# A two-layer decoder trunk: X by two DMA queues, a new plan for the convolution's taps, one sum in layer 1's norm

## The chip, the cores and the metric

One core of one Trainium2 chip runs the whole computation. The metric is the device time of one execution in microseconds; lower is better. The times are of three runs of the kernel before, and the profile is of one more execution.

## The reference

x is 256 tokens by 1024 channels, float32. Two layers, both with a residual.

```python
# layer 0
h = rms_norm(x, norm0_g)
a, bv, bg, z = split(h @ w_in0)            # 1024, 1024, 1024, 2048 columns
ya = (multiscale_pool(a) @ pool_w per group) * pool_scale
u  = causal_depthwise_conv(bv * sigmoid(bg), conv_w, 31 taps) + conv_b
yb = silu(layer_norm(u, cnorm_g, cnorm_b))
x  = x + (concat(ya, yb) * silu(z)) @ w_out0
# layer 1
h = rms_norm(x, norm1_g)
q, k, v, z = split(h @ w_in1)              # 4 x 1024 columns
q, k = rms_norm per head of 64, q * 64 ** -0.5
o = softmax(q k' - slope * distance, causal) v   # 16 heads; 256 tokens are one block
x = x + (o * silu(z)) @ w_out1
```

rms_norm divides by sqrt(mean(x * x) + 1e-6) over the 1024 channels.

## The kernel before, in words

**Units.** All weights come as 49 units of 128 x 2048 float32 (1 MB) in the order of use: 0 to 7 the gate and value of the convolution in turn, 8 to 11 the pooling channels, 12 to 15 and 17 to 20 the SiLU gates of layer 0 (`ZB`, `ZA`), 16 the pooling weights (`PW`), 21 to 28 the output projection (`OA`, `OB`), 29 to 32 the gate of layer 1 (`Z1`), 33 to 44 k, q and v in pairs, 45 to 48 the last projection. A float32 product is made of three fp32r matmuls: weights and activations are cut into a rounded high part (`w_hi`, `h_hi`, by ScalarE, `cut_hi`, L461) and the rest (`w_lo`, `h_lo`, by VectorE, `cut_lo`, L740), and `product` (L1077 to L1079) adds hi*hi, hi*lo and lo*hi. Five units, `NATIVE`, are multiplied uncut in float32, and the low part of four units, `ADDED`, is made by an accumulating DMA that GpSimd issues (L426) after ScalarE has written minus the high part.

**Buffers and queues.** `raw` holds four units. SyncE issues the loads in order (L399), each as soon as the unit four before it has been cut. w_hi and w_lo hold four cuts. Each engine runs one fixed instruction list, and semaphores order them. X (128 partitions x 8 tiles of 256) comes first on SyncE's queue, in two DMAs of four tiles each (L388), the units follow, and the parameters (149 KB, norm gains and convolution taps) go by ScalarE's queue (L494).

**Start.** TensorE runs 12 warm-up matmuls on a tile of ones (L1145). ScalarE squares X by pairs of tiles, TensorE adds the squares over partitions by eight matmuls with the ones (L1154), ScalarE takes the root, VectorE the reciprocal (`take_inverse`). Before that VectorE multiplies X by the gain (`gained`, L746), and unit 0 works on this product, without the reciprocal; its result is scaled late (`late_gate`, `scale_late`, named in `EARLY`). Unit 1 is the first to need the normed h.

**Convolution.** 31 taps on 8 tiles of channels run on VectorE in the slots of units 2 to 21, placed ahead of time by `conv_plan`: a tap is either one multiply-add of VectorE a tile (L856), or a product that ScalarE makes for two tiles (L548) and VectorE adds (L860), or, for two pairs, an accumulating DMA of GpSimd. The planner goes slot by slot with a budget: the unit's length less what `slot_work` says that each engine has to do there already; it gives a product to ScalarE where its budget is over 0.8. The products of late slots live in a ring of four. After the last tap VectorE folds eight tiles into one (L873), TensorE adds over partitions (L1200, `MEAN_AT`), VectorE centres (L880), ScalarE squares (L469), VectorE folds again (`fold`, L767), and TensorE makes the sum at `SUM2_AT` (L1154). ScalarE casts unit 26 ahead of these squares.

**Layer 1's norm.** As the last projection of layer 0 closes two tiles at a time, VectorE adds the residual (L961), applies the gain (L746) and makes the low part (`low_h(1, m)`, L753); ScalarE squares (L469) and makes the high part (L487). In the loop over `Z1`, units 29 and 30 work on the h without the reciprocal, in ya_hi and ya_lo, and are scaled late; unit 31 is the first that needs `over_rms`, which norms H and cuts it again. The sum over partitions is four matmuls inside unit 29: after step k = 1 the two tiles that hold folded pairs, after k = 2 the two last tiles unfolded.

## Time and profile before

| | us |
|---|---|
| median of 3 runs (lowest to highest) | 329.43 (329.25 to 330.02) |
| the profiled execution | 329.37 |
| its span, first to last instruction | 327.4 |
| TensorE busy (matmul / weight load) | 321.8 / 295.5 |
| VectorE busy | 261.1 |
| ScalarE busy | 235.8 |
| GpSimd busy | 51.2 |
| TensorE's granted clock, mean | 0.999 of full |

The span is what the profile covers; the execution's own time has some 2 us around it. A row of the timeline gives start, length, engine, line, what is written from what, and how many instructions are merged into it; the brackets give idle time before it and who ended it. A float32 matmul has two records, an fp32r matmul one.

### The profile page before, as it was taken

Reading aid. Unit: us, or ns where it says so; the run is one execution under the profiler, and the core shown is the slowest. Engines: PE = TensorE matmul, PEld = TensorE weight load, DVE = VectorE, ACT = ScalarE, POOL = GpSimd, SP = SyncE. Lnnn points to the kernel's source line nnn. Section 1 sums busy time; section 2 is a strip of 40 time slices with the busy share of each in tenths; the row PEclk is TensorE's granted clock in tenths of the full one; section 3 lists DMA queues with packets and bytes.
Section 4 is the critical chain, followed back from the end, with each engine's and each line's share of the span. In section 5 each row is a group of like instructions: output and inputs, shape, how many; then the busy total and the mean of one; then the engine's idle time right before and its main releaser. Section 6 shows DMA issues by size and latency. Waiting matters only on the chain.

```text
span 327.4 us, 5849 instructions
## 1 busy us (share of the span) xinstructions
PE 321.8 (98%) x2244; PEld 295.5 (90%) x2244; DVE 261.1 (80%) x482; ACT 235.8 (72%) x436; POOL 51.2 (16%) x58
## 2 busy tenths in 40 slices
PE   8999999999999999998999999999999999999995
PEld 8899999999999999997999999988887777778885
DVE  2799989999999999999895898846556887758533
ACT  4687999997999889987766557814756667566630
POOL 0050024423224112120000000005500231400000
PEclk9999999999999999999999999999999999999999
DMA  7988478969999699984539244780635323200003
GB/s 275 413 278 355 156 265 224 203 148 344 346 328 214 122 411 292 217 270 93 249 143 397 104 148 152 279 322 13 243 130 166 132 103 129 114 2 0 2 0 130
DMA packets 12843, 64.79 MB, mean 198 GB/s; under 512 B 1424, under 2 KB 1552, under 8 KB 6544
## 3 DMA queue, kind: packets, MB, share of 16 engines
q1 hardware_dynamic: 8064, 53.78, 43.3%
q0 software_dynamic: 4608, 10.49, 17.7%
q8 instruction: 18, 0.29, 0.4%
q10 hardware_dynamic: 144, 0.15, 0.2%
q14 instruction: 9, 0.07, 0.1%
HBM read 52.88 MB, written 1.05 MB: 165 GB/s over the span
## 4 chain that ended last, share of the span: by engine, by line
PE 90%; ACT 4%; DVE 3%; issue 1%; POOL 0%; DVEq 0%; ACTq 0%; POOLq 0%
PE bank L1077 24%; PE bank L1078 23%; PE bank L1079 23%; PE bank L1111 4%; PE bank L1137 3%; PE bank L1185 2%; PE bank L1291 2%; PE bank L1318 2%; PE bank L1154 2%; PE bank L1145 2%; PE bank L1304 2%; ACT scratch L548 1%; DVE scratch L856 1%; ACT w_hi L461 1%; PE bank L1270 1%
## 5 line engine op out<-in xcount | busy, mean ns | idle before, releaser
L740 DVE TENSOR_TENSOR w_lo<-raw,w_hi 128x1024 fp32r<-128x1024 f32 x80 | 95.3, 1222 | 16.9 <-ACT w_hi L461 16.7
L461 ACT CAST w_hi<-raw 128x1024 fp32r<-128x1024 f32 x88 | 88.6, 1047 | 7.5 <-DMA raw<-w 3.8
L1077 PE MATMUL bank<-h_hi,w_hi 128*128 128x256 f32 x320 | 91.1, 285 | 0.0
L1079 PE MATMUL bank<-h_hi,w_lo 128*128 128x256 f32 x320 | 90.5, 283 | 0.0
L1078 PE MATMUL bank<-h_lo,w_hi 128*128 128x256 f32 x320 | 90.5, 283 | 0.0
L1078 PEld LDWEIGHTS bank<-h_lo,w_hi 128*128 128x128 f32 x320 | 61.4, 192 | 0.1
L1077 PEld LDWEIGHTS bank<-h_hi,w_hi 128*128 128x128 f32 x320 | 61.4, 192 | 0.1
L1079 PEld LDWEIGHTS bank<-h_hi,w_lo 128*128 128x128 f32 x320 | 61.4, 192 | 0.0
L856 DVE SCALAR_TENSOR_TENSOR scratch<-scratch,params 128x256 f32<-128x256 f32 x106 | 43.4, 482 | 0.2
L1077 PE MATMUL bank<-ya_hi,w_hi 128*128 128x256 f32 x144 | 42.6, 296 | 0.0
L1078 PE MATMUL bank<-ya_lo,w_hi 128*128 128x256 f32 x144 | 40.7, 282 | 0.0
L1079 PE MATMUL bank<-ya_hi,w_lo 128*128 128x256 f32 x144 | 40.7, 282 | 0.0
L1077 PE MATMUL bank<-w_hi,h_hi 128*128 128x512 f32 x96 | 39.2, 408 | 0.0
L1078 PE MATMUL bank<-w_lo,h_hi 128*128 128x512 f32 x96 | 37.6, 391 | 0.0
L1079 PE MATMUL bank<-w_hi,h_lo 128*128 128x512 f32 x96 | 37.5, 391 | 0.0
L548 ACT ACTIVATE scratch<-scratch,params 128x256 f32<-128x256 f32 x78 | 32.8, 504 | 0.0
L435 POOL DMA_DIRECT2D side_v<-side_ring x24 | 21.0, 905 | 73.9 <-ACT side_ring L528 52.8
L1077 PEld LDWEIGHTS bank<-ya_hi,w_hi 128*128 128x128 f32 x144 | 27.5, 191 | 2.0 <-issue 1.7
L1078 PEld LDWEIGHTS bank<-ya_lo,w_hi 128*128 128x128 f32 x144 | 27.5, 191 | 0.1
L1079 PEld LDWEIGHTS bank<-ya_hi,w_lo 128*128 128x128 f32 x144 | 27.5, 191 | 0.0
L860 DVE TENSOR_TENSOR scratch<-scratch 128x512 f32<-128x512 f32 x39 | 26.1, 690 | 1.0
L446 POOL TENSOR_SCALAR scratch<-scratch 128x8 f32<-128x8 f32 x8 | 5.1, 632 | 116.5 <-DVE scratch L1037 116.2
(106 smaller groups left out, 522.2 us busy)
## 6 DMA issues: line engine op xcount, KB each, us to landing
raw<-w SPq DMA_DIRECT2D x49, 1024.0 KB, 6.9
side_v<-side_ring POOLq DMA_DIRECT2D x24, 256.0 KB, 6.5
w_lo<-raw POOLq DMA_DIRECT2D x8, 512.0 KB, 7.3
X<-xT SPq DMA_DIRECT2D x2, 512.0 KB, 5.2
out<-X SPq DMA_DIRECT2D x4, 256.0 KB, 2.6
consts<-const SPq DMA_DIRECT2D x1, 290.0 KB, 13.3
params<-vec ACTq DMA_DIRECT2D x1, 149.0 KB, 4.9
```

Source lines behind the costliest of these rows:

```text
L435: pool.dma_start(side_v[:, pair, item % 2, :, :], side_home(pair, item), accum_op=ALU.add).then_inc(side_added[pair][item % 2], 16)
L461: nc.scalar.copy(halves(w_hi, cut_slot(n), half), halves(raw, n % RAW, half)).then_inc(hi_cut, 1)
L548: last = nc.scalar.mul(product_home(product)[:, i, :], U[:, c, k:k + S], column(CW + TAPS * c + k))
L740: nc.vector.tensor_tensor(halves(w_lo, cut_slot(n), half), halves(raw, n % RAW, half), halves(w_hi, cut_slot(n), half).bitcast(F32), ALU.s ...
L856: nc.vector.scalar_tensor_tensor(V[:, c, :], U[:, c, k:k + S], column(CW + TAPS * c + k), V[:, c, :], ALU.mult, ALU.add).then_inc(tap, 1)
L860: nc.vector.tensor_tensor(V[:, c:c + 2, :], V[:, c:c + 2, :], product_home(product), ALU.add).then_inc(tap, 1)
L1077: nc.tensor.matmul(dst, wh, ah, start=start, stop=False, skip_group_check=True)
L1078: nc.tensor.matmul(dst, wh, al, start=False, stop=False, skip_group_check=True)
L1079: return nc.tensor.matmul(dst, wl, ah, start=False, stop=stop, skip_group_check=True)
L1111: last = nc.tensor.matmul(dst, wr, (H if n else H0)[:, k, :], start=start, stop=stop, skip_group_check=True)
L1137: return nc.tensor.matmul(dst, wr, SZ[:, (KD if n in OB else 0) + tile, :], start=start and m % 2 == 0, stop=stop, skip_group_check=True)
L1145: nc.tensor.matmul(bank[7][:, 0:P], ones[:, :], ones[:, :], start=True, stop=True, skip_group_check=True)
```

## The change

X comes in two DMAs by partition halves, one issued by SyncE, one by ScalarE, on one semaphore; each partition's 8 KB is one piece. The parameters are issued by ScalarE after its half. Both engines wait for all of X. The warm-up has 10 matmuls. In the planner `ZA[3]` is given 1.2 less of VectorE work, `PW` 0.8 less of ScalarE work, and from `ZA[3]` on products go to ScalarE only after four entries of the slot. Layer 1's squares are folded to one tile, in two parts, and summed by one matmul after k = 5. Unit 31 joins the units that work without the reciprocal. Unit 32's high cast, and those of 33 and 34, come sooner in ScalarE's list; VectorE cuts 33 and 34 before unit 31's late gate.

```diff
--- before.py
+++ after.py
@@ -57,7 +57,7 @@
 EARLY_ADDED = (10,)
 ADDED = EARLY_ADDED + (21, 22, 24)
 SPARE = 22
-WARM = 12
+WARM = 10
 RAW = 4
 CUT = 4
 
@@ -123,6 +123,8 @@
     return sum(1 for n in units[:i] if n not in NATIVE)
 
 
+
+SQUARE_FOLDS = (0, 2, 2, 2), (0, 4, 2, 3), (0, 6, 2, 4), (0, 1, 1, 4)
 
 STEPS = 48
 CUT_HI_AT, CUT_LO_AT = (1, 7, 9, 15), (2, 8, 11, 15)
@@ -185,8 +187,10 @@
         dve, act = dve + 0.8, act + 0.6
     if n in BG or n in A or n in ZB or n in ZA:
         act += 0.6
+    if n == ZA[3]:
+        dve -= 1.2
     if n in (ZB[0], PW):
-        act += 0.7 if n == ZB[0] else 1.6
+        act += 0.7 if n == ZB[0] else 0.8
     return dve, act
 
 
@@ -212,7 +216,7 @@
                 late = len(used)
             free = pair < (n - 1) // 2
             last_ones = n == OA[0] and sum(map(len, left.values())) <= LAST_PRODUCTS
-            if last_ones or act_time > 0.8 and free and n < OA[0] and n + 3 != SPARE:
+            if last_ones or act_time > 0.8 and free and n < OA[0] and n + 3 != SPARE and (n < ZA[3] or len(plan[n]) >= 4):
                 count += 1
                 plan[n].append((tiles, k, len(used), max(last.get(c, 0) for c in tiles), count))
                 used.append(count)
@@ -239,8 +243,9 @@
 
 
 MEAN_AT = 2, 0, 5
+SUM3_AT = 5
 SUM2_AT = 3, 0, 2
-EARLY = (BG[0],), (Z1[0], Z1[1])
+EARLY = (BG[0],), (Z1[0], Z1[1], Z1[2])
 
 
 def hybrid_trunk(nc, xT, w, vec, const, out):
@@ -326,7 +331,7 @@
         TR, SC, PV = bank[4], (bank[5], bank[6]), bank[7]
 
 
-        x_in = [sem(f"x_in{i}") for i in range(2)]
+        x_in = sem("x_in")
         vec_in, const_in, stored = sem("vec_in"), sem("const_in"), sem("stored")
         raw_in = [sem(f"raw_in{i}") for i in range(RAW)]
         ones_set, pads_set, qs_set = sem("ones_set"), sem("pads_set"), sem("qs_set")
@@ -384,8 +389,7 @@
 
         @block.sync
         def _(sp):
-            for i in range(2):
-                sp.dma_start(X[:, 4 * i:4 * i + 4, :], xT[:, 4 * i:4 * i + 4, :]).then_inc(x_in[i], 16)
+            sp.dma_start(X[0:P // 2, :, :], xT[0:P // 2, :, :]).then_inc(x_in, 16)
             for n in range(NU):
                 m = n - RAW
                 if m >= 0:
@@ -491,12 +495,13 @@
                 act.wait_ge(late, layer + i + 1)
                 nc.scalar.activation(dst, dst, func).then_inc(done, 1)
 
+            act.dma_start(X[P // 2:P, :, :], xT[P // 2:P, :, :]).then_inc(x_in, 16)
             act.dma_start(V_[:, :], vec).then_inc(vec_in, 16)
             act.wait_ge(ones_set, 2)
             prime(ACT.Sqrt)
             for m in range(4):
-                if m % 2 == 0:
-                    act.wait_ge(x_in[m // 2], 16)
+                if m == 0:
+                    act.wait_ge(x_in, 32)
                 square(0, m, X)
             take_root(bank[4], 1)
             prime(ACT.Sigmoid)
@@ -625,10 +630,13 @@
                 high_h(1, m)
             cut_hi(Z1[1])
             take_root(bank[0], 3)
+            prime(ACT.Silu)
             cut_hi(Z1[2])
+            cut_hi(Z1[3])
             for m in range(4):
                 high_h(2, m)
-            cut_hi(Z1[3])
+            cut_hi(KU[0])
+            cut_hi(KU[0] + 1)
 
             def head_exp(h):
 
@@ -665,8 +673,6 @@
                             heads_hi(4 * octet + i)
 
             for i, n in enumerate(Z1):
-                if i > 1:
-                    cut_hi(n + 2)
                 to = SZ1[:, 2 * i:2 * i + 2, :]
                 if n in EARLY[1]:
                     late_gate(1, i, to, ACT.Silu, sz1_ready)
@@ -755,14 +761,12 @@
 
             folds = 0
 
-            def fold(group, pairs):
+            def fold(group, first, last):
 
                 nonlocal folds
-                steps = ((0, 2, 2), (0, 4, 2), (0, 6, 2), (0, 1, 1)) if pairs == 4 else ((0, 2, 2), (0, 4, 2))
-                for i, (a, b, n) in enumerate(steps):
-                    if i < 3:
-                        dve.wait_ge(sq_ready, 4 * group + i + 2)
-                    if i:
+                for a, b, n, squares in SQUARE_FOLDS[first:last]:
+                    dve.wait_ge(sq_ready, 4 * group + squares)
+                    if first or (a, b) != SQUARE_FOLDS[first][:2]:
                         dve.wait_ge(folded, folds)
                     nc.vector.tensor_tensor(SQ[:, a:a + n, :], SQ[:, a:a + n, :], SQ[:, b:b + n, :],
                                             ALU.add).then_inc(folded, 1)
@@ -795,8 +799,8 @@
 
             dve.wait_ge(vec_in, 16)
             for m in range(4):
-                if m % 2 == 0:
-                    dve.wait_ge(x_in[m // 2], 16)
+                if m == 0:
+                    dve.wait_ge(x_in, 32)
                 gained(0, m)
             take_inverse(1)
             normed_h(0, 0)
@@ -914,7 +918,7 @@
                     low_ya(i)
 
             centre()
-            fold(1, 4)
+            fold(1, 0, 4)
             cut_lo(OB[1], (0,))
             take_inverse(2)
             dve.wait_ge(sq_ready, 8)
@@ -967,10 +971,12 @@
                     residual(m, 0)
                     dve.wait_ge(x_updated, m + 1)
                     gained(1, m)
+                if m == 4:
+                    fold(2, 2, 4)
                 if m:
                     low_h(1, m - 1)
                 if m == 2:
-                    fold(2, 3)
+                    fold(2, 0, 2)
             cut_lo(Z1[1])
             take_inverse(3)
             cut_lo(Z1[2])
@@ -1025,11 +1031,11 @@
                         if s == values[i] + 3:
                             heads_lo(4 * octet + i)
 
-            for i, n in enumerate(Z1):
-                if i > 1:
-                    cut_lo(n + 2)
-                if n in EARLY[1]:
-                    scale_late(1, i, SZ1[:, 2 * i:2 * i + 2, :])
+            for i, n in enumerate(EARLY[1]):
+                if i == 2:
+                    cut_lo(KU[0])
+                    cut_lo(KU[0] + 1)
+                scale_late(1, i, SZ1[:, 2 * i:2 * i + 2, :])
 
             def qk_sums(r):
 
@@ -1253,11 +1259,9 @@
                 if n % 4 == 0:
                     pe.wait_ge(root_ready, 3)
                 for k in range(KD):
-                    channel_step(n, k, {Z1[0]: 1, Z1[2]: 2}.get(n))
-                    if n == Z1[0] and k == 1:
-                        square_sums(6, (0, 1), bank[0], False)
-                    if n == Z1[0] and k == 2:
-                        square_sums(0, (6, 7), bank[0], True)
+                    channel_step(n, k, {Z1[0]: 1, Z1[3]: 2}.get(n))
+                    if n == Z1[0] and k == SUM3_AT:
+                        square_sums(8, (0,), bank[0], True)
 
             def turn_qk(octet, isq, half):
 
```

## Rows read from the trace of the kernel before

**Rows 1.** The page, part 1: busy us (share of the span) xinstructions.
```profile
PE 321.8 (98%) x2244; PEld 295.5 (90%) x2244; DVE 261.1 (80%) x482; ACT 235.8 (72%) x436; POOL 51.2 (16%) x58
```
**Rows 2.** Waits of TensorE: engine line waited for: us in total, times, longest.
```profile
PE bank L1200 <- DVE scratch L873: 0.8, 1, 0.8
```
**Rows 3.** Timeline of the start, 0 to 26 us.
```profile
0.98 5.36 PE L1145 MATMUL bank<-ones 128*128 128x128 f32 x24 [0.98 <-POOL eps L411]
...
5.47 1.15 ACT L469 ACTIVATE scratch<-X 128x512 f32<-128x512 f32 x2 [2.81 <-DMA X<-xT]
5.64 2.27 DVE L746 TENSOR_SCALAR scratch<-X,params 128x256 f32<-128x256 f32 x8 [5.64 <-DMA params<-vec]
...
6.18 3.70 PE L1154 MATMUL bank<-scratch,ones 128*128 128x256 f32 x16
...
9.71 7.07 PE L1111 MATMUL bank<-scratch,raw 128*128 128x256 f32 x32
...
10.42 1.75 DVE L773 RECIPROCAL rinv<-root 128x256 f32<-128x256 f32 x1 [2.50 <-ACT root L473]
...
15.15 1.29 DVE L753 TENSOR_TENSOR h_lo<-H,h_hi 128x512 fp32r<-128x512 f32 x2
...
16.43 0.47 PE L1077 MATMUL bank<-h_hi,w_hi 128*128 128x256 f32 x1
```
**Rows 4.** Layer 1's norm: chain in order of time, then VectorE's timeline.
```profile
186.09 0.86 PE bank L1154 x4
186.95 0.12 PE bank L1077
...
186.31 1.47 DVE L753 TENSOR_TENSOR ya_lo<-H,ya_hi 128x512 fp32r<-128x512 f32 x2
...
205.07 4.74 DVE L740 TENSOR_TENSOR w_lo<-raw,w_hi 128x1024 fp32r<-128x1024 f32 x4 [1.64 <-ACT w_hi L461]
```
**Rows 5.** Timeline of VectorE and ScalarE, slots 19 to 21, 120 to 150 us.
```profile
127.27 4.05 DVE L856 SCALAR_TENSOR_TENSOR scratch<-scratch,params 128x256 f32<-128x256 f32 x10
...
133.96 4.69 DVE L860 TENSOR_TENSOR scratch<-scratch 128x512 f32<-128x512 f32 x6
...
143.92 2.50 DVE L860 TENSOR_TENSOR scratch<-scratch 128x512 f32<-128x512 f32 x4
...
132.96 4.90 ACT L548 ACTIVATE scratch<-scratch,params 128x256 f32<-128x256 f32 x12
```
**Rows 6.** Layer 0's second sum: chain, then timeline, 120 to 178 us.
```profile
155.25 0.54 PE bank L1154 x2
...
149.91 2.48 DVE L880 TENSOR_TENSOR scratch<-scratch,bank 128x512 f32<-128x512 f32 x4 [0.25 <-PE bank L1200]
152.31 2.74 DVE L767 TENSOR_TENSOR scratch<-scratch 128x512 f32<-128x512 f32 x4
...
148.74 1.99 ACT L461 CAST w_hi<-raw 128x1024 fp32r<-128x1024 f32 x2 [2.63 <-issue]
150.64 2.42 ACT L469 ACTIVATE scratch<-scratch 128x512 f32<-128x512 f32 x4
...
122.82 1.05 ACT L461 CAST w_hi<-raw 128x1024 fp32r<-128x1024 f32 x1 [1.10 <-PE bank L1079]
```
**Rows 7.** Issues of X, ns and start; us to landing; parameters and constants.
```profile
L388 SPq DMA_DIRECT2D X<-xT x2: 373/400/426, 0.7 to 1.1; - x2
DMA to landing us min/median/max: 4.7/5.2/5.6
...
params<-vec ACTq DMA_DIRECT2D x1, 149.0 KB, 4.9
...
consts<-const SPq DMA_DIRECT2D x1, 290.0 KB, 13.3
```
**Rows 8.** The load of a unit issued at 190.4, L399.
```profile
DMA to landing us min/median/max: 4.7/4.7/4.7
```
**Rows 9.** Window 5 to 6 us: busy by engine, granted clock, DMA share, GB/s.
```profile
5.00:6.00 1.00, 1.00 (x6) 1.00 (x6) 0.36 (x2) 0.53 (x1) 0.00 (x0) 1.00 1.06 435
```

## Prediction

> **What bounds the kernel now.** I read the page's busy times first, then TensorE's waits, then the start and the two norms in the timeline. TensorE is busy 321.8 of 327.4 us [rows 1]. Its one wait for another engine is 0.8 us at L1200, for VectorE's folded mean [rows 2]; the rest of its idle time is the 0.98 us before its first instruction and the last residual add and store. So the time falls only by what TensorE no longer does, by that one wait, or by an earlier start, and it rises by any new wait of TensorE.
>
> The start is a chain, not a busy engine. The warm-up matmuls run from 0.98 for 5.36 us, ScalarE squares the first half of X at 5.47 (it had waited for the transfer), the eight sums start at 6.18 and unit 0 follows at 9.71 with no wait between [rows 3]. TensorE is then continuous to the wait at L1200, and the first unit that needs the norm starts at 16.43.
>
> The profiled execution took 329.37 us, span and what lies around it; the median of the runs is 329.43, so I sum against 329.37 and add 0.06.
>
> **Part 1: one sum in layer 1's norm instead of four.** The four fp32 sums stand in the chain as two pieces of 0.86 us, two sums each [rows 4]: 0.43 us a sum. Three of them go: 3 x 0.43 = 1.29 us of TensorE time in a stretch with no wait. That is the whole gain if the one sum finds its operand.
>
> VectorE gets a third add over 512 columns and a fourth over 256, before its last h_lo. Before, the two last h_lo run from 186.31 for 1.47 us [rows 4]. After, in the clock of before: h_lo 186.31, third add 186.9 (the squares end 186.4), fourth 187.7 to 188.1, last h_lo 188.05 to 188.75. TensorE's unit 29 starts at 184.5, a channel step is six matmuls of 0.12 us [rows 4] = 0.72, so the sum after step 5 is reached at 184.5 + 6 x 0.72 = 188.8, and step 6, which needs the last h_lo, at 189.2. Slack 0.7 and 0.45 us. Unit 30's low half is ready at 189.9 and used at 190.7. The root is 0.5 later than before, and over_rms now has one unit (48 x 0.12 = 5.8 us) more, because unit 31 no longer needs it. I take 1.29; bounds 0 (TensorE waits as long as it saved) and 1.3.
>
> Casts of 33 and 34: before, the four low halves of units 33 and 34 run from 205.07 to 209.8, after 1.64 us of waiting for ScalarE, while TensorE reaches unit 33 at about 209.2 [rows 4]. TensorE comes 1.29 sooner now, so these would be the next late thing if they stayed. They move: ScalarE cuts both right after the last h_hi (about 200 to 204), VectorE after two late gates (203.2 to 207.9). Needed: the first halves at 207.9, ready by 206.7. Their raw buffers are read sooner, so the loads four units later go out sooner, never later. The slots are free at the ends of units 29 and 30 (190.7 and 196.4). Unit 31's late gate comes behind on VectorE (to 208.5) and its bank is wanted two units of attention later. The Silu table load only changes place. Cost 0; bounds 0 and 0.5 if one cast is late.
>
> **Part 2: the plan of the convolution.** The planner's arithmetic, done with the new terms, changes three slots. Slot 16 has one more product from ScalarE for two taps of VectorE; slot 19 two more taps; slot 20 begins with four taps ahead of its six products; slot 21 has six taps where there were ten. A tap is 4.05/10 = 0.40 us, an add of a product 2.50/4 = 0.62 or a little less when the product is there, but 4.69/6 = 0.78 in slot 20, where VectorE keeps step with ScalarE's 4.90/6 = 0.82 a product [rows 5]. With four taps ahead (1.6 us) the products are there: six adds save about 6 x 0.2 = 1.2; slot 16 saves 2 x 0.40 - 0.60 = 0.2. The taps moved from 20 and 21 to 19 cancel. The ring of four products holds ScalarE up by 0.4 us in slot 20; its last product of slot 21 comes at about 144.1, and VectorE wants it at 144.3. So the folded mean is ready 1.4 us sooner, against a wait of 0.8: that wait goes. In slot 16 ScalarE's extra 0.8 us falls in its wait for unit 16.
>
> What is late next is layer 0's second sum. It takes 0.54 us in the chain where a sum is 0.43, so TensorE already waits 0.1 there for the fold [rows 6]. The fold starts at 152.31, after the centring (149.91, 2.48 us) and after the second square. The centring follows TensorE's mean and comes 0.85 sooner. The squares don't: ScalarE first casts unit 26 at 148.74 for 1.99 us, behind a wait for that unit's load [rows 6], and squares from 150.64. Its second square ends at 151.86, so the fold starts at 151.9: 0.4 sooner. The load hangs on the accumulating transfers of unit 22, which go back to ScalarE's cast at 122.82, released by TensorE after 1.10 us of waiting [rows 6], and so keep step with TensorE. So of the wait of 0.85, I take 0.45 us as won (0.4, and a little for the 0.2 that VectorE is ahead), bounds 0 (load 0.4 later) and 0.95 (load 0.5 sooner). What follows, root, gates and OB, keeps its distance from this sum.
>
> **Part 3: the input.** Both halves of X were issued at 0.7 and 1.1 and landed after 4.7 and 5.6 us: 5.4 and 6.7 [rows 7]. ScalarE starts 0.05 after the first, TensorE's sums 0.7 after that. Now all of X must land. The trace has no X in 8 KB packets, but a load of a unit, 1024 KB in 128 pieces of 8 KB, issued alone at 190.4, took 4.7 us [rows 8]; from 0.7 that is 5.4, where the first half was. So nothing is won or lost: 0. Bounds: landing at 5.0 (each queue only has to issue half), 0.4 won; landing at 6.35, that is 6.7 less the 149 KB of parameters that no longer run beside it at 0.43 MB/us [rows 9], 0.9 lost. The warm-up, 24 records of 0.22 us, loses four and ends at 5.3: it would allow 0.86 and costs nothing, since it waits for X; it does not itself win anything.
>
> The Trainium skill, page "DMA: Bandwidth & Descriptors", section "Rules for kernel authors", advises against two transfers to disjoint partition halves, because they share the same 16 DMA engines and serialize. No row here shows it; by it the landing goes from 5.4 toward rival A.
>
> The parameters now stand behind ScalarE's half of X and run beside unit 0's load. Taking turns by packet, their 149 KB pass with about 1 MB of the load: 1.15 MB at 0.43 MB/us = 2.7 us after X, so 8.2 instead of 5.6. VectorE's gains take 2.27 us and end at 10.5; its reciprocal started at 10.42 [rows 3]. The first h_lo pair starts 15.15, the first is done at 15.8 and TensorE wants it at 16.4: 0.5 us of slack hides this. Unit 0 wants the first gain at 9.7 and gets it at 8.9. Cost 0 up to a landing at 8.7, and then one for one.
>
> **The sum.** 1.29 + 0.45 + 0 = 1.74; 329.37 - 1.74 = 327.63, with the 0.06: 327.7 us.
>
> **Rivals.**
> A. X lands as late as its second half did, less the parameters (6.35). For it: at the kernel's start 512 KB and the parameters took the 4.7 us that 1024 KB took at 190.4 [rows 7, 8], so the start may be slow whatever the packets. Against: with packets of twice the size the same pieces at the same pace carry the whole of X. Gain 1.74 - 0.93 = 0.8: 328.6 us. The rule quoted above is this rival. Chance 0.14.
> B. Slower: the parameters are not given turns but stand behind the four unit loads of SyncE's queue. The constants, the next in that queue, land at 4.2 + 13.3 = 17.5 [rows 7]; less their own 290 KB the parameters would come at about 16.7, unit 0 at 17.4 instead of 9.7: 7.7 - 1.74 = 6.0 slower, 335.3 us. It costs from a landing at 8.7 and turns the sum at 10.4. Against it: before, the parameters landed at 0.7 + 4.9 = 5.6 [rows 7], between two halves of X from the other queue. Chance 0.04.
> C. X at 5.0 and the wait at L1200 gone whole: 1.29 + 0.95 + 0.4 = 2.64, 326.8 us. For it: the transfers before unit 26's load are all ScalarE's to send. Chance 0.14.
> D. The load of unit 26 gets no better and slips behind: nothing of the wait is won. 1.29: 328.1 us. Chance 0.10.
> E. The one sum or the last h_lo is late by more than the 0.5 to 0.7 of slack, or 33 and 34 are, and part 1 gives nothing: 0.45, 329.0 us. Chance 0.08.
> The forecast as it stands: 0.50.
>
> **Range and chances.** 0.2% is 0.66 us, about what a measurement tells from no change. Cases forecast, A, C and D are faster by more than that (0.88), E lies at the edge and gives 0.03 to faster and 0.05 to no change; B is slower. Faster 0.91, same 0.05, slower 0.04. The range runs from C to beyond A: 326.7 to 328.8, and leaves out E and B. The forecast's own is 327.2 to 328.1.
>
> **What would show it.** The line L1200 gone from TensorE's waits, and a wait or a stretched piece at L1154 near 154.5; one piece of 0.43 where two of 0.86 stood; TensorE's sums starting within 0.2 us of 6.18; VectorE's gains starting near 8.2 and ending before 10.6; the adds of slot 20 at 0.6 each; units 33 and 34 cast before unit 32 ends. I am wrong if the first unit after the norm starts other than 16.4 by more than 0.5, or if TensorE waits anywhere between 184 and 220.

## The result and the profile after

The changed kernel took 332.23 us (median of 6 runs, 331.27 to 333.87), the kernel before 329.44 beside it: a ratio of 1.0089, 95% interval 1.0073 to 1.0104. It is slower by 2.8 us where the forecast was 1.7 us faster. The profiled execution took 332.21 us.

The page's span and busy times answer to [rows 1]:

```profile
span 330.4 us, 5837 instructions
PE 321.9 (97%) x2234; PEld 295.0 (89%) x2234; DVE 261.4 (79%) x484; ACT 236.5 (72%) x439; POOL 48.0 (15%) x58
PEclk9699999999999999999999999999999999999999
```

TensorE has ten matmul records less (four for two warm-up matmuls, six for three sums; a float32 matmul has two) and is as busy as before, in a span 3 us longer. So something of TensorE's became slower, and the clock row names the place: a 6 in the second slice (8.3 to 16.5 us). TensorE's waits on other engines (in total, times, longest) answer to [rows 2]:

```profile
PE bank L1160 <- ACT scratch L473: 3.7, 1, 3.7
```

The wait of 0.8 at L1200 is gone (the line is L1206 now), and one of 3.7 us at the very first sums has come. The timeline of the start answers to [rows 3]:

```profile
0.98 3.85 PE L1151 MATMUL bank<-ones 128*128 128x128 f32 x20 [0.98 <-POOL eps L415]
8.53 6.45 PE L1160 MATMUL bank<-scratch,ones 128*128 128x256 f32 x16 [3.70 <-ACT scratch L473]
...
14.82 7.07 PE L1117 MATMUL bank<-scratch,raw 128*128 128x256 f32 x32
...
21.54 0.47 PE L1083 MATMUL bank<-h_hi,w_hi 128*128 128x256 f32 x1
...
7.85 2.19 ACT L473 ACTIVATE scratch<-X 128x512 f32<-128x512 f32 x4 [4.17 <-DMA X<-xT]
...
10.96 2.19 DVE L752 TENSOR_SCALAR scratch<-X,params 128x256 f32<-128x256 f32 x8 [10.96 <-DMA params<-vec]
15.53 1.75 DVE L777 RECIPROCAL rinv<-root 128x256 f32<-128x256 f32 x1 [2.38 <-ACT root L477]
```

Unit 0 starts at 14.82 where it started at 9.71: 5.11 us late, in two parts. The sums start at 8.53 instead of 6.18 (2.35), and they take 6.45 instead of 3.70 (2.75). The DMA issues (KB, us from issue to landing) answer to [rows 7]:

```profile
X<-xT SPq DMA_DIRECT2D x1, 512.0 KB, 4.7
X<-xT ACTq DMA_DIRECT2D x1, 512.0 KB, 7.1
...
params<-vec ACTq DMA_DIRECT2D x1, 149.0 KB, 9.6
```

SyncE's half landed at 5.4, ScalarE's, issued at the same time, at 7.8. By window (busy share with instructions of PE, PEld, DVE, ACT, POOL; then the granted clock, the DMA share, GB/s), to stand against [rows 9]:

```profile
4.00:5.00 1.00, 0.83 (x8) 0.64 (x6) 0.00 (x0) 0.00 (x0) 0.00 (x0) 1.00 0.94 213
5.00:6.00 1.00, 0.00 (x0) 0.00 (x0) 0.00 (x0) 0.00 (x0) 0.00 (x0) 1.00 1.00 213
6.00:7.00 1.00, 0.00 (x0) 0.00 (x0) 0.00 (x0) 0.00 (x0) 0.00 (x0) 1.00 1.07 229
7.00:8.00 1.00, 0.00 (x0) 0.00 (x0) 0.00 (x0) 0.15 (x1) 0.00 (x0) 0.63 0.84 299
8.00:9.00 1.00, 0.47 (x1) 0.47 (x2) 0.00 (x0) 1.00 (x3) 0.00 (x0) 0.50 1.09 437
...
13.00:14.00 1.00, 1.00 (x4) 0.82 (x3) 0.15 (x1) 0.00 (x0) 0.00 (x0) 0.50 1.00 418
14.00:15.00 1.00, 1.00 (x6) 0.90 (x5) 0.00 (x0) 0.00 (x0) 0.00 (x0) 0.95 0.97 401
```

Two things are to be read here. From 4 to 7 us the DMA engines are busy throughout (share 0.94 to 1.07; it can read a little over 1) and move 213 to 229 GB/s; before, the window 5 to 6 had 435 at the same share. And the halves come one after the other. Each line gives a queue's DMA pieces that start in a window, their MB, and their time as a share of the 16 engines': SyncE's queue (q1) from 2 to 3 us, then ScalarE's (q10) from 5 to 6, each alone in its window:

```profile
q1 hardware_dynamic: 36, 0.29, 100.3%
q10 hardware_dynamic: 26, 0.21, 100.3%
```

The 26 pieces of 8 KB fill 16 engines for 1 us: 0.62 us a piece. TensorE, idle from 4.8 on, loses its clock in the window 7 to 8, runs its sums at 0.50 (1.2 GHz) and has full clock (2.4 GHz) again only as they end.

The middle and layer 1's norm, in VectorE's and ScalarE's timelines and then two pieces of the chain of waits, answer to [rows 4 to 6]:

```profile
139.55 1.67 DVE L860 SCALAR_TENSOR_TENSOR scratch<-scratch,params 128x256 f32<-128x256 f32 x4
141.14 3.69 DVE L864 TENSOR_TENSOR scratch<-scratch 128x512 f32<-128x512 f32 x6
...
153.94 2.48 DVE L884 TENSOR_TENSOR scratch<-scratch,bank 128x512 f32<-128x512 f32 x4 [0.47 <-PE bank L1206]
156.47 2.81 DVE L771 TENSOR_TENSOR scratch<-scratch 128x512 f32<-128x512 f32 x4
...
153.39 1.99 ACT L465 CAST w_hi<-raw 128x1024 fp32r<-128x1024 f32 x2 [1.56 <-issue]
...
203.65 3.88 ACT L465 CAST w_hi<-raw 128x1024 fp32r<-128x1024 f32 x4
```
```profile
159.33 0.70 PE bank L1160 x2
...
193.21 0.43 PE bank L1160 x2
```

Slot 20's adds take 0.61 each, as forecast. ScalarE's cast of unit 26 starts 4.65 later than before where all else starts 5.11 later: it gained 0.46 on the rest. One sum of 0.43 stands where two pieces of 0.86 stood. The ends of units in TensorE's stream put it all in one table (us; the last column is what the stage won or, negative, lost):

| end of unit | before | after | difference | won in the stage |
|---|---|---|---|---|
| 0 | 16.78 | 21.89 | +5.11 | -5.11 |
| 22 | 145.77 | 150.88 | +5.11 | 0 |
| 24 | 160.47 | 164.71 | +4.24 | 0.87 |
| 28 | 184.65 | 188.89 | +4.24 | 0 |
| 29 | 192.11 | 195.07 | +2.96 | 1.28 |
| last | 323.68 | 326.64 | +2.96 | 0 |

### The profile page after: what moved, and what is told of

Its sections match the earlier page's. It is cut to its first block, busy times and chain, and to the rows that moved or that the text cites. A ratio compares the mean times of both kernels' runs of the same rounds, so it can differ in the third digit from the quotient of the medians.

```text
span 330.4 us, 5837 instructions
## 1 busy us (share of the span) xinstructions
PE 321.9 (97%) x2234; PEld 295.0 (89%) x2234; DVE 261.4 (79%) x484; ACT 236.5 (72%) x439; POOL 48.0 (15%) x58
## 3 DMA queue, kind: packets, MB, share of 16 engines
HBM read 52.88 MB, written 1.05 MB: 163 GB/s over the span
## 4 chain that ended last, share of the span: by engine, by line
PE 87%; DMA 6%; ACT 3%; issue 1%; DVE 1%; DVEq 0%; ACTq 0%; SPq 0%
PE bank L1083 24%; PE bank L1085 23%; PE bank L1084 23%; PE bank L1117 4%; DMA w_lo<-raw 2%; PE bank L1160 2%; DMA X<-xT 2%; PE bank L1143 2%; PE bank L1191 2%; PE bank L1295 2%; PE bank L1322 2%; ACT w_hi L465 2%; DMA raw<-w 2%; PE bank L1308 2%; PE bank L1274 1%
## 5 line engine op out<-in xcount | busy, mean ns | idle before, releaser
L1083 PE MATMUL bank<-h_hi,w_hi 128*128 128x256 f32 x304 | 86.6, 285 | 0.0
L1085 PE MATMUL bank<-h_hi,w_lo 128*128 128x256 f32 x304 | 86.0, 283 | 0.0
L1084 PE MATMUL bank<-h_lo,w_hi 128*128 128x256 f32 x304 | 86.0, 283 | 0.0
L1083 PEld LDWEIGHTS bank<-h_hi,w_hi 128*128 128x128 f32 x304 | 58.3, 192 | 0.1
L1085 PEld LDWEIGHTS bank<-h_hi,w_lo 128*128 128x128 f32 x304 | 58.3, 192 | 0.0
L1083 PE MATMUL bank<-ya_hi,w_hi 128*128 128x256 f32 x160 | 46.9, 293 | 0.0
L1085 PE MATMUL bank<-ya_hi,w_lo 128*128 128x256 f32 x160 | 45.2, 283 | 0.0
L1084 PE MATMUL bank<-ya_lo,w_hi 128*128 128x256 f32 x160 | 45.2, 282 | 0.0
L1083 PEld LDWEIGHTS bank<-ya_hi,w_hi 128*128 128x128 f32 x160 | 30.6, 191 | 2.0 <-issue 1.7
L1083 PEld LDWEIGHTS bank<-w_hi,h_hi 128*128 128x128 f32 x96 | 18.0, 188 | 5.6 <-issue 2.3
```

The source lines that it names most:

```text
L1083: nc.tensor.matmul(dst, wh, ah, start=start, stop=False, skip_group_check=True)
L1084: nc.tensor.matmul(dst, wh, al, start=False, stop=False, skip_group_check=True)
L1085: return nc.tensor.matmul(dst, wl, ah, start=False, stop=stop, skip_group_check=True)
```

## The experiments

**Theory.** The whole loss is the input. A transfer that writes only partitions 0 to 63, or only 64 to 127, moves at half the pace, and the two run in turn; TensorE's longer idle time then costs it its clock through the sums. **Rivals.** Two queues slow each other whatever they carry; the second queue starts late at the launch; the 8 KB pieces are the matter; X's place in memory is; or part of the loss comes from the plan and layer 1. The diffs below are against the changed kernel unless the text says against the kernel before. The ratio is to the kernel before, on the same chip. In experiments 1 to 3 and 5, 19 executions of the kernel before have a median of 329.52 us, and one of them took 332.83; there the recorded ratio and the ratio of the medians lie apart by up to 0.3%, and the second is given where it matters.

**1. All but the input and the warm-up.**
```diff
-            sp.dma_start(X[0:P // 2, :, :], xT[0:P // 2, :, :]).then_inc(x_in, 16)
+            for i in range(2):
+                sp.dma_start(X[:, 4 * i:4 * i + 4, :], xT[:, 4 * i:4 * i + 4, :]).then_inc(x_in[i], 16)
-            act.dma_start(X[P // 2:P, :, :], xT[P // 2:P, :, :]).then_inc(x_in, 16)
-WARM = 10
+WARM = 12
```


> The changed kernel with the input, the parameters' place and the 12 warm-up matmuls of before. Theory: all of the loss lies in the start (unit 0 ended 5.11 us later in the changed kernel), and the rest won 2.15 us (0.87 at layer 0's mean and second sum, 1.28 at layer 1's sum). Expected 329.4 - 2.15 = 327.3 us. Rival, that the plan or the casts gain only because the start was late (the load of unit 26 had more time): layer 0's part gives the forecast's 0.45 and the time is 327.7.

326.94 us, ratio 0.9898 (0.9853 to 0.9943; by the medians 0.992, or 2.6 us): the lowest median of the study, below the 327.3 expected. Units 0, 24, 29 and the last end at 16.68, 159.35, 189.71 and 321.28, so against before the start won 0.10, the middle 1.02 and layer 1 1.28. ScalarE's timeline shows where the middle won more than forecast:

```profile
147.83 1.99 ACT L466 CAST w_hi<-raw 128x1024 fp32r<-128x1024 f32 x2 [1.23 <-issue]
```

It started at 148.74 before [rows 6]: 0.91 sooner.

**2. The input alone.** Against the kernel before: the two half transfers, one semaphore, `WARM = 10`, nothing else.
```diff
-            for i in range(2):
-                sp.dma_start(X[:, 4 * i:4 * i + 4, :], xT[:, 4 * i:4 * i + 4, :]).then_inc(x_in[i], 16)
+            sp.dma_start(X[0:P // 2, :, :], xT[0:P // 2, :, :]).then_inc(x_in, 16)
+            act.dma_start(X[P // 2:P, :, :], xT[P // 2:P, :, :]).then_inc(x_in, 16)
```


> The kernel before with only the changed input (two halves by partitions, parameters behind, 10 warm-ups). Theory: the loss is the input's alone, 329.4 + 5.1 = 334.5 us, with unit 0 starting near 14.8 and the wait at L1200 as before. Rival, that the old plan's VectorE was late enough to hide some of it: 333.6 or less.

334.58 us, ratio 1.0124 (1.0076 to 1.0171; by the medians 1.015, or 5.1 us). Unit 0 ends at 21.96 (5.18 late), the last at 328.83 (5.15 late): all of it arises before unit 0. TensorE's waits:

```profile
PE bank L1154 <- ACT scratch L468: 3.4, 1, 3.4
PE bank L1200 <- DVE scratch L873: 0.8, 1, 0.8
```

The new wait of the start stands beside the old one of the middle. The two parts of the change are separate, and the input alone is the loss.

**3. The price of the clock.** The warm-up is made long enough to reach X's landing, so TensorE has next to no idle time.
```diff
-WARM = 10
+WARM = 18
```


> The changed kernel with 18 warm-up matmuls in place of 10. Theory: TensorE's idle 3.7 us (4.83 to 8.53) let its clock fall to 0.50, and the eight sums took 6.45 us where they took 3.70; with matmuls up to about 8.6 the clock stays at 1.00, the sums take 3.7 and the time is 332.2 - 2.7 = 329.5 us, X landing as late as before (7.8). Rival, that what ends last is VectorE's gains, started by the parameters at 10.96 and ending at 13.15: then unit 1 starts later than the sums allow and the gain is only 1 to 2 us, 330.2 to 331.2.

329.54 us, ratio 0.9989 (0.9969 to 1.0009): 2.7 us come back. X landed no sooner:

```profile
0.98 7.19 PE L1151 MATMUL bank<-ones 128*128 128x128 f32 x36 [0.98 <-POOL eps L415]
8.55 3.72 PE L1160 MATMUL bank<-scratch,ones 128*128 128x256 f32 x16 [0.37 <-ACT scratch L473]
```

The sums start where they did (8.55) and take 3.72 again. So 2.7 of the 5.1 us is the clock, and the other 2.4 the late landing of X. The mean granted clock of executions that were not profiled fits in most: 0.990 to 0.995 in four of the changed kernel's other five, 0.997 or more in all ten here. One of the changed kernel's has 1.000 and took 332.15 us all the same, which this account leaves open.

**4. One transfer over all partitions.** The same 8 KB pieces, all from SyncE; ScalarE issues the parameters alone; `WARM = 12`.
```diff
-            sp.dma_start(X[0:P // 2, :, :], xT[0:P // 2, :, :]).then_inc(x_in, 16)
+            sp.dma_start(X[:, :, :], xT[:, :, :]).then_inc(x_in, 16)
-            act.dma_start(X[P // 2:P, :, :], xT[P // 2:P, :, :]).then_inc(x_in, 16)
```


> The changed kernel with all of X in one transfer over 128 partitions on SyncE's queue, the same 8 KB pieces, the parameters alone on ScalarE's queue, 12 warm-ups. Theory (write side: a transfer over one half of the partitions runs at half rate): pieces of about 310 ns, X lands near 5.4, the sums start at 6.1 to 6.3, 326.9 to 327.3 us, as with the input of before. Rival (8 KB pieces of X are slow at the kernel's start, whoever writes them): pieces of 600 ns, X after 7.5, 331 us or more.

327.76 us, ratio 0.9942 (0.9927 to 0.9957). The issue and a window:

```profile
X<-xT SPq DMA_DIRECT2D x1, 1024.0 KB, 5.5
```
```profile
5.00:6.00 1.00, 1.00 (x6) 1.00 (x6) 0.00 (x0) 0.00 (x0) 0.00 (x0) 1.00 1.08 443
```

443 GB/s with 8 KB pieces: their size is not the matter. A piece takes half the time, too. From 6 to 7 us, when q1 alone moves the first unit's load over all partitions:

```profile
q1 hardware_dynamic: 54, 0.44, 104.3%
```

That is 0.31 us a piece, against 0.62 in the changed kernel. X landed at 6.2, not at the 5.4 expected, and the time missed the expected range by 0.5 us. The parameters (q10) moved beside it, and from 2 to 3 us the engines moved only 99 GB/s at a share of 0.30; how much each cost isn't shown.

**5. Each queue over both sides.** SyncE takes partitions 32 to 95, ScalarE 0 to 31 and 96 to 127; `WARM = 12`.
```diff
-            sp.dma_start(X[0:P // 2, :, :], xT[0:P // 2, :, :]).then_inc(x_in, 16)
+            sp.dma_start(X[32:96, :, :], xT[32:96, :, :]).then_inc(x_in, 16)
-            act.dma_start(X[P // 2:P, :, :], xT[P // 2:P, :, :]).then_inc(x_in, 16)
+            for a in (0, 96):
+                act.dma_start(X[a:a + 32, :, :], xT[a:a + 32, :, :]).then_inc(x_in, 16)
```


> The changed kernel with the partitions of X shared out otherwise: SyncE's queue loads partitions 32 to 95, ScalarE's 0 to 31 and 96 to 127, in the same 8 KB pieces, with 12 warm-ups. Theory 1, a transfer that writes only partitions 0 to 63 or only 64 to 127 reaches half of the write paths (its pieces took about 600 ns instead of 309): now each queue covers both sides, X lands by 5.5 to 6.0 and the time is 327.3 to 327.9 us. Theory 2, the loss is that two queues take turns, or that 64 pieces in a row come from one contiguous 512 KB: pieces of 600 ns again, X at 7.8 and 331 to 332 us.

328.46 us, ratio 0.9967 (0.9942 to 0.9993): between the halves and the whole, a miss on time. The rate from 2 to 7 us was 270, 303, 328, 229 and 358 GB/s. ScalarE's two transfers still write one side each, and the theory had to be put more narrowly: what one transfer covers is what counts. This run fits that, and doesn't test it by itself. The sums:

```profile
7.43 3.72 PE L1161 MATMUL bank<-scratch,ones 128*128 128x256 f32 x16 [1.75 <-ACT scratch L473]
```

An idle time of 1.75 us left them at full clock in this execution. Two of the ten took 330.18 and 330.19 us with a mean clock of 0.995 instead of 0.999 to 1.000; they weren't profiled.

**6. Two queues, each over all partitions.** The halves are cut by tile instead (4 KB pieces); `WARM = 12`.
```diff
-            sp.dma_start(X[0:P // 2, :, :], xT[0:P // 2, :, :]).then_inc(x_in, 16)
+            sp.dma_start(X[:, 0:4, :], xT[:, 0:4, :]).then_inc(x_in, 16)
-            act.dma_start(X[P // 2:P, :, :], xT[P // 2:P, :, :]).then_inc(x_in, 16)
+            act.dma_start(X[:, 4:8, :], xT[:, 4:8, :]).then_inc(x_in, 16)
```


> The changed kernel with X halved by tiles as before (128 partitions, 4 KB pieces), one half by each queue, one semaphore, the parameters behind, 12 warm-ups. Theory (write side): two queues as such cost nothing, X lands by 5.6 to 6.2, 327.1 to 327.7 us. Rival (the second queue is served after the first): X after 6.8, 328.2 us or more.

327.33 us, ratio 0.9928 (0.9913 to 0.9943), as expected. ScalarE's transfer and a window:

```profile
X<-xT ACTq DMA_DIRECT2D x1, 512.0 KB, 4.9
```
```profile
4.00:5.00 1.00, 1.00 (x10) 1.00 (x10) 0.00 (x0) 0.00 (x0) 0.00 (x0) 1.00 1.08 442
```

Two queues at once are not the matter, nor does ScalarE's begin late: 4.7 and 4.9 us, at 442 GB/s.

**7. The halves from one queue.** Both from SyncE, one after the other, parameters alone from ScalarE; `WARM = 12`.
```diff
+            sp.dma_start(X[P // 2:P, :, :], xT[P // 2:P, :, :]).then_inc(x_in, 16)
...
-            act.dma_start(X[P // 2:P, :, :], xT[P // 2:P, :, :]).then_inc(x_in, 16)
```


> The changed kernel with both partition halves of X on SyncE's queue, one after the other, the parameters alone on ScalarE's queue, 12 warm-ups. Theory (write side): each half runs at half rate wherever it is issued, X lands at 7.3 to 7.9; with the warm-up to 6.2 TensorE is idle for less than 2 us and its clock stays up, so 328.8 to 329.5 us, and the parameters land near 5.6. Rival (the loss was the turn of the second queue): X lands near 5.4 and the time is 327.0 us.

332.24 us, ratio 1.0077 (1.0061 to 1.0094). Slow without a second queue for X, which the theory wants; but I had expected X not later than in the changed kernel and the clock kept, at 328.8 to 329.5 us. Why X came a microsecond later than by two queues isn't shown. Windows, then the sums:

```profile
4.00:5.00 1.00, 1.00 (x7) 1.00 (x7) 0.00 (x0) 0.00 (x0) 0.00 (x0) 1.00 0.66 148
5.00:6.00 1.00, 1.00 (x7) 1.00 (x6) 0.00 (x0) 0.00 (x0) 0.00 (x0) 1.00 0.96 238
```
```profile
9.64 5.22 PE L1160 MATMUL bank<-scratch,ones 128*128 128x256 f32 x16 [3.39 <-ACT scratch L474]
```

The parameters landed first, after 2.9 us, and X was used only at 8.96. Idle 3.39 us, and again the clock falls to 0.50 before the sums start; it is 1.00 again from 13 us.

**8. The plan alone.** Against the kernel before: the planner's two terms and its condition on slots from `ZA[3]` on, as in the change's diff.
```diff
+    if n == ZA[3]:
+        dve -= 1.2
...
-        act += 0.7 if n == ZB[0] else 1.6
+        act += 0.7 if n == ZB[0] else 0.8
```


> The kernel before with only the three edits of the convolution's plan. Theory: the wait at L1200 goes and the second sum comes 0.9 to 1.1 us sooner, because unit 26's load, too, lands that much sooner (with the input of before ScalarE cast it at 147.83 where it was 148.74): 329.5 - 1.0 = 328.5 us. Rival, the forecast's: the load keeps its time and only 0.45 is won, 329.1 us.

328.48 us, ratio 0.9972 (0.9961 to 0.9983), as expected. The wait for the folded mean is gone. Unit 22 ends at 146.16 (0.39 late, as is unit 0 in this execution) and unit 24 at 159.78 (0.69 early): 1.08 us won in the middle.

**9. Layer 1 alone.** Experiment 1 without the planner's edits.
```diff
-    if n == ZA[3]:
-        dve -= 1.2
...
-        act += 0.7 if n == ZB[0] else 0.8
+        act += 0.7 if n == ZB[0] else 1.6
```


> The changed kernel with the input and the plan of before: only layer 1's norm, casts and late gate are changed. Theory: three fp32 sums at 0.43 us, 329.5 - 1.3 = 328.2 us, with the wait of 0.8 us at L1200 still there. Rival: the casts of 33 and 34 won something of their own, 328.0 or less; or the earlier parts add up differently, and the plan alone and this one do not sum to the 2.6 us of the two together.

328.01 us, ratio 0.9955 (0.9943 to 0.9967). The wait of the middle is back, and unit 26's cast starts at 149.32 where it started at 148.74 before, 0.6 later; units 24 and 29 end at 160.62 and 190.99, the second 1.27 us nearer the first than before. The wait, then ScalarE's cast:

```profile
PE bank L1204 <- DVE scratch L875: 0.8, 1, 0.8
```
```profile
149.32 1.99 ACT L464 CAST w_hi<-raw 128x1024 fp32r<-128x1024 f32 x2 [3.24 <-issue]
```

**10. Halves by every second partition.** 64 partitions and 8 KB pieces a queue, as in the change, but even and odd; `WARM = 12`.
```diff
+            sp.dma_start(X[0:P:2, :, :], xT[0:P:2, :, :]).then_inc(x_in, 16)
...
+            act.dma_start(X[1:P:2, :, :], xT[1:P:2, :, :]).then_inc(x_in, 16)
```


> The changed kernel with SyncE loading the even and ScalarE the odd partitions of X, 12 warm-ups. Both queues now span all partitions in every stretch, with 64 pieces of 8 KB each as in the changed kernel. Theory (write side): X lands by 5.4 to 5.8 and the time is 326.9 to 327.5 us; the parameters still come after, near 8.2, hidden by slack. Rival (two queues in turn, or 64 pieces a transfer): X after 7 and 329.5 us or more.

327.68 us, ratio 0.9939 (0.9923 to 0.9956), 0.2 above the expected range.

```profile
4.00:5.00 1.00, 1.00 (x7) 1.00 (x7) 0.00 (x0) 0.00 (x0) 0.00 (x0) 1.00 0.96 401
5.00:6.00 1.00, 1.00 (x7) 0.85 (x6) 0.00 (x0) 0.00 (x0) 0.00 (x0) 1.00 0.97 405
```

The number of partitions and the queues are the change's own, and the rate is 401 to 405 where the change had 213. What matters is which partitions. X landed 4.2 and 5.4 us after issue, at 6.1, and the sums started at 6.88: still 0.7 later than before, where they could start on the first half of X, and 1.65 sooner than in the change.

**11. Tiles 0 and 1 first**, parameters first from ScalarE, `WARM = 10`: a try to start the sums sooner.
```diff
+            for i, (a, b) in enumerate(((0, 2), (2, 8))):
+                sp.dma_start(X[:, a:b, :], xT[:, a:b, :]).then_inc(x_in[i], 16)
```


> The changed kernel with X on SyncE's queue in two transfers over 128 partitions, the first two tiles (256 KB) and then the other six, the parameters first on ScalarE's queue, 10 warm-ups. Theory: the first pair lands by 4.9, the sums start near 5.5 instead of 6.15, unit 0 near 9.1, held by its load (landed at 9.2 before): 326.94 - 0.3 to 0.6 = 326.3 to 326.6 us. Rival: the small first transfer pays the same 4.7 us to landing as a half, nothing is won, 326.9 us; or the second part is then late (6.2, as one transfer was) and holds the sums of tiles 2 and 3, 327.2 us.

327.98 us, ratio 0.9971 (0.9952 to 0.999). The rival was right that the rest would be late, after 6.1 us, but its 327.2 was still too low.

```profile
5.98 1.13 PE L1160 MATMUL bank<-scratch,ones 128*128 128x256 f32 x4 [0.36 <-ACT scratch L474]
7.97 2.86 PE L1160 MATMUL bank<-scratch,ones 128*128 128x256 f32 x12 [0.86 <-ACT scratch L474]
```

The first sums started 0.2 us sooner than in experiment 1, and unit 0 1.05 later (10.66 against 9.61). The second sum of the middle waited too, for 0.7 us, since unit 26's cast came at 149.91. The profiled execution took 328.75 us; seven of the twelve took 328.07 or less, so this wait needn't be in all.

**12. Four pairs of tiles, in turn on two queues**, parameters behind, `WARM = 10`.
```diff
+            for i in (0, 2):
+                sp.dma_start(X[:, 2 * i:2 * i + 2, :], xT[:, 2 * i:2 * i + 2, :]).then_inc(x_in[i], 16)
...
+            for i in (1, 3):
+                act.dma_start(X[:, 2 * i:2 * i + 2, :], xT[:, 2 * i:2 * i + 2, :]).then_inc(x_in[i], 16)
```


> The changed kernel with X in four transfers of two tiles over 128 partitions, in turn by SyncE's and ScalarE's queue, each with its own semaphore, the parameters behind ScalarE's, 10 warm-ups. Theory: the first pair lands by 4.9 and the sums start near 5.5, but the parameters land near 7.7 to 8.9 and VectorE's gains end at 11.1, so the reciprocal is 0.6 to 0.7 later than in the version with the input of before and the slack of 0.5 us before unit 1 is used up: 326.7 to 327.1 us. Rival: the parameters are hidden altogether, 326.3 us.

328.54 us, ratio 0.9964 (0.9954 to 0.9973): a miss. The sums started at 5.41, but the parameters were late now, and the cover that the prediction counts on was gone. TensorE's wait, then VectorE:

```profile
PE bank L1119 <- DVE scratch L754: 1.0, 1, 1.0
```
```profile
10.16 2.19 DVE L754 TENSOR_SCALAR scratch<-X,params 128x256 f32<-128x256 f32 x8 [10.16 <-DMA params<-vec]
```

Unit 0 waited 1.0 us for the gains.

**13 and 14. Written side or read side.** In the changed kernel each half also reads its own half of X in memory. x's rows are laid out so that in 13 each queue writes a half of the partitions and reads every second 8 KB, and in 14 each writes every second partition and reads half of the memory in one stretch; three executions each.
```diff
+            sp.dma_start(X[0:P // 2, :, :], xT[0:P:2, :, :]).then_inc(x_in, 16)      # 13
+            act.dma_start(X[P // 2:P, :, :], xT[1:P:2, :, :]).then_inc(x_in, 16)     # 13
...
+            sp.dma_start(X[0:P:2, :, :], xT[0:P // 2, :, :]).then_inc(x_in, 16)      # 14
+            act.dma_start(X[1:P:2, :, :], xT[P // 2:P, :, :]).then_inc(x_in, 16)     # 14
```


> The changed kernel, but x lies in memory with the rows of the two halves in turn, so that each queue writes partitions 0 to 63 or 64 to 127 as in the changed kernel and reads every second 8 KB of the whole megabyte. Theory (write side): nothing changes, ScalarE's half lands after about 7 us, about 220 GB/s from 4 to 6 us, 332 us. Rival (read side: 512 KB that lie together are read at half rate): X lands by 5.5 to 6.2 and the time is 328 us.

> The counterpart: SyncE's queue writes the even and ScalarE's the odd partitions, but each reads 512 KB that lie together, as in the changed kernel; 10 warm-ups. Theory (write side): about 400 GB/s from 4 to 6 us, X lands near 6.1 as with odd and even partitions before, 327.7 to 328.0 us. Rival (read side): about 220 GB/s, X near 7.8, 332 us.

13 took 332.18 us, ratio 1.008 (1.0056 to 1.0105); 14 took 327.54, ratio 0.9938 (0.9915 to 0.996). Windows of 13, windows of 14, and the sums of 13:

```profile
4.00:5.00 1.00, 1.00 (x7) 1.00 (x7) 0.00 (x0) 0.00 (x0) 0.00 (x0) 1.00 0.95 213
5.00:6.00 1.00, 0.62 (x3) 0.33 (x2) 0.00 (x0) 0.00 (x0) 0.00 (x0) 1.00 1.07 229
```
```profile
4.00:5.00 1.00, 1.00 (x8) 1.00 (x7) 0.00 (x0) 0.00 (x0) 0.00 (x0) 1.00 1.01 401
5.00:6.00 1.00, 0.27 (x3) 0.08 (x1) 0.00 (x0) 0.44 (x1) 0.00 (x0) 1.00 0.98 384
```
```profile
8.66 5.41 PE L1160 MATMUL bank<-scratch,ones 128*128 128x256 f32 x16 [3.04 <-ACT scratch L473]
```

The pace follows the partitions written, not the memory read. The pair also gives the cleanest price: the same ten warm-up matmuls, two queues, pieces and one wait for all of X, and the sums start at 8.66 in 13 and at 6.25 in 14, 2.4 us apart.

## Why the prediction was wrong

**Part 3, the input, failed.** The step was "a load of a unit, 1024 KB in 128 pieces of 8 KB, issued alone at 190.4, took 4.7 us [...] So nothing is won or lost: 0", with 0.9 us as the worst bound. That row has the changed kernel's size and number of pieces but writes all 128 partitions in one transfer. Each transfer of the change writes one half, and at 213 to 229 GB/s 512 KB take about 2.4 us: just the distance from SyncE's landing (5.4) to ScalarE's (7.8). Experiments 4, 6 and 10 keep in turn the piece size, the two queues and the 64 partitions, and all reach 401 to 443 GB/s; 13 and 14 exclude the memory side; 7 excludes two queues as the cause. So the cause is shown. The sums started 2.35 us later than before. Against experiment 10 the halves account for 1.65 of it, and the other 0.7 goes with waiting for all of X, which the prediction also had at nothing; between 13 and 14 the halves alone make 2.4. The two pairs differ, and the split is known only within these bounds.

Rival A, the rule on two transfers to disjoint halves (the Trainium skill, page "DMA: Bandwidth & Descriptors", section "Rules for kernel authors"), went the right way, and I gave it 0.14. I priced it from rows on whole transfers in a row (6.35); the landing was 7.8. The range was therefore too narrow at this end by construction: both of its bounds took the old rate as given. The Trainium skill, page "SBUF — State Buffer", section "Door 1: The DMA port swizzle (why `[64,N]` ≈ `[32,N]`)", holds what was needed: partitions 0 to 63 reach 8 of 16 ports, with some 218 GB/s as the limit against 436 for all 128. The windows agree within some 5% (213 to 229 GB/s against 401 to 443).

**The clock was in no term.** The step "The warm-up [...] loses four and ends at 5.3: it would allow 0.86 and costs nothing, since it waits for X" takes an idle TensorE for free. The warm-up ended at 4.83, not 5.3, and X came 2.4 us late. Idle from 4.8 on, it ran its sums at granted clock 0.50 and lost 2.75 us; experiment 3 gets 2.7 back with a longer warm-up and X as late as ever. The two together are the 5.1 us between forecast and result at unit 0. "I am wrong if the first unit after the norm starts other than 16.4 by more than 0.5": it started at 21.54.

**The parameters** landed at 10.9, not at 8.2, since they stood behind a half that was itself late, and the gains ended at 13.15, beyond the 11.0 (a landing at 8.7 and 2.27 us of gains) from which I had them cost. They cost nothing here, where the sums ended only at 15.0, and nothing in experiment 3 either, where the sums ended at 12.3 and TensorE's only wait for another engine behind its warm-up is the 0.37 us for X. In experiment 12, with sums that ended at 9.9, they cost 1.0. Rival B did not come: they waited neither for four loads nor to 16.7.

**Part 1 was right.** Forecast 1.29; measured 1.28 here and in experiment 1, 1.27 in experiment 9. The piece of 0.43 stands, TensorE waits for no engine from 184 to 220, and units 33 and 34 are cast in one stretch of ScalarE. Rival E did not come.

**Part 2 was right in its mechanism, mis-sized.** Forecast 0.45; measured 0.87 here, 1.02 in experiment 1, 1.08 in experiment 8. The wait at L1200 is gone and the second sum does wait a little (a piece of 0.70 at 159.33). The term that was off is the time of unit 26's load, which was taken to keep its distance from TensorE ("so keep step with TensorE"): ScalarE's cast of it began 0.46 us nearer the rest here and 0.91 sooner in experiment 1. The traces show that the load was issued only a little sooner and landed faster. Before it was issued at 141.4 and landed after 7.3 us; in experiment 1 at 141.2 and after 6.5, in experiment 8 at 141.5 and after 6.7, in the change at 146.2 (0.3 sooner, less the 5.11) and after 7.1. In experiment 9, without the planner's edits, it took 7.6; but in experiments 11 and 12, with them, 7.2 and 7.3, and there the second sum waited 0.7 and 0.6. So that the edits alone make this load faster isn't shown; these are single executions, and what moved beside the load hasn't been compared.

With part 3 at nothing, the forecast of 1.74 would have stood against 2.40 measured by unit ends in experiment 1 (0.10 + 1.02 + 1.28). That is rival C's mechanism in the middle, without the 0.4 it wanted at the start; its time was 326.8 and experiment 1 measured 326.94. Agreement with this rival's total is partly luck, since its parts came out otherwise. The version to keep is that one: the change with the input of before, 2.6 us under the kernel before on the same chip and 5.3 under the changed one. None of the other inputs beat it (327.3 to 328.5 in experiments 4, 5, 6, 10, 11, 12 and 14), though experiment 6 (327.33, on another chip) can't be told apart from it: the intervals of the two ratios overlap.

## What to carry to other kernels

Before a transfer is priced by another of its size, compare which partitions the two write: the row must match the destination's span as well as the bytes and the piece. Where the DMA share is full and GB/s is half of what the same share moved elsewhere in the profile, look at the partitions before the queues. The first microsecond of traffic is no measure for this: the kernel before, which writes all partitions, moved 174 GB/s at a share of 1.00 from 2 to 3 us. And price a transfer on which TensorE waits twice: once for the wait, and, if the wait is as long as the 3 us and more seen here, once for what runs behind it at the lower clock.

## What the runs showed of the hardware

- Transfers over partitions 0 to 63 or 64 to 127 moved at 213 to 229 GB/s from 4 to 6 us with the DMA engines all busy, from two queues (the change, experiment 13), and at 148 to 238 from one (experiment 7, where the share was 0.66 in the slowest window). A piece of 8 KB took 0.62 us in the change from 5 to 6 us, and 0.31 over all partitions (experiment 4). Two such transfers issued at once, one to each half, did not add up: they ran one after the other, and their landings lay 2.4 us apart.
- 64 partitions as such are not slow: even and odd partitions by two queues moved at 401 to 405 GB/s (experiment 10) and 384 to 401 (14). The Trainium skill, page "SBUF — State Buffer", section "Can I just issue two DMAs to hit both halves?", says no for the two halves, and the change agrees; it goes on that only one transfer over all 128 partitions reaches all 16 ports. Two transfers of 64 partitions each moved nearly twice the rate of the halves here, so in this the runs differ, and the measurement decides.
- After idle times of TensorE of 3.70, 3.4, 3.39 and 3.04 us (the change, experiments 2, 7, 13) its granted clock went from 1.00 to 0.50 (2.4 to 1.2 GHz), and the sums took 5.2 to 6.7 us instead of 3.7. In the first three it fell before the sums started; in 13 it was still 1.00 in the window 8 to 9, 0.82 in 9 to 10 and 0.50 in 10 to 11, with the sums running from 8.66. After 1.75 and 0.98 us (the profiled executions of experiments 5 and 14) it kept 1.00. What lies between was not tried.
